# The second layer's gate and up gemms of a two-block transformer kernel, 256 tokens per matmul instead of 512

## What is computed

```python
h = rmsnorm(x, norm2_g[i]) * (1.0 + sc2) + sh2
x = x + g2 * swiglu(h, w_gate[i], w_up[i], w_down[i])

def swiglu(h, w_gate, w_up, w_down):
    return (jax.nn.silu(h @ w_gate) * (h @ w_up)) @ w_down
```

## Time and profile before

| What | Value |
|---|---|
| Median of 3 runs | 2285.78 us |
| Lowest and highest | 2285.34 us, 2288.35 us |
| Profiled execution, first to last instruction (its span) | 2283.5 us |
| PE busy | 2243.0 us, 98% of the span |
| PEld (weight loads) busy | 1801.7 us, 79% |
| DVE busy | 1190.3 us, 52% |
| ACT busy | 897.0 us, 39% |
| POOL busy | 164.5 us, 7% |
| Mean granted TensorE clock | 0.996 of full speed |

### The profile page before, as it was taken

How to read it: one execution, slowest core, us unless ns; L and a number is a source line. 1 busy time by engine, 2 the same in 40 slices (tenths; PEclk the granted TensorE clock), 3 DMA queues, 4 the chain that set the end, 5 groups by cost and what they waited for, 6 DMA issues and landing times. The chain is left out here.

```text
span 2283.5 us, 27109 instructions
## 1 busy us (share of the span) xinstructions
PE 2243.0 (98%) x11012; PEld 1801.7 (79%) x11012; DVE 1190.3 (52%) x1642; ACT 897.0 (39%) x1446; POOL 164.5 (7%) x147
## 2 busy tenths in 40 slices
PE   7999999999999999999999999999999999999998
PEld 4767788888777778888888878887788888888886
DVE  4765755543465754333336546567752346553453
ACT  3664322232354533322234236377653224331331
POOL 2112000000100010000001001032110001000001
PEclk9999999999999999999999999999999999999999
DMA  9322555532211122222222324333233222323222
GB/s 347 129 102 103 196 206 216 203 111 102 84 65 65 56 74 84 101 93 93 101 92 83 111 84 139 118 109 111 97 103 122 90 102 84 110 87 107 93 83 83
DMA packets 82172, 259.11 MB, mean 113 GB/s; under 512 B 8800, under 2 KB 17248, under 8 KB 82048
## 3 DMA queue, kind: packets, MB, share of 16 engines
q1 hardware_dynamic: 82048, 257.38, 32.6%
HBM read 253.09 MB, written 4.26 MB: 113 GB/s over the span
## 5 line engine op out<-in xcount | busy, mean ns | idle before, releaser
L850 PE MATMUL pb<-hhi,whi 128*128 128x512 f32 x1944 | 771.8, 397 | 3.0 <-ACT hhi L1263 3.0
L852 PE MATMUL pb<-hhi,wlo 128*128 128x512 f32 x1944 | 757.9, 390 | 2.3 <-DVE wlo L1534 2.3
L854 PE MATMUL pb<-hlo,whi 128*128 128x512 f32 x1944 | 758.5, 390 | 0.0
L1534 DVE TENSOR_TENSOR wlo<-raw,whi 128x1024 fp32r<-128x1024 f32 x361 | 446.5, 1241 | 536.4 <-ACT whi L1225 536.2
L1225 ACT ACTIVATE whi<-raw 128x1024 fp32r<-128x1024 f32 x361 | 380.2, 1057 | 699.2 <-PE pb L854 679.1
L850 PEld LDWEIGHTS pb<-hhi,whi 128*128 128x128 f32 x1944 | 365.0, 188 | 90.7 <-issue 17.2
L852 PEld LDWEIGHTS pb<-hhi,wlo 128*128 128x128 f32 x1944 | 365.3, 188 | 79.1 <-DVE wlo L1534 3.1
L854 PEld LDWEIGHTS pb<-hlo,whi 128*128 128x128 f32 x1944 | 364.8, 188 | 78.8 <-DVE hlo L1631 0.9
L850 PE MATMUL pb<-ahi,whi 128*128 128x512 f32 x848 | 335.0, 395 | 1.4 <-ACT ahi L1421 0.7
L852 PE MATMUL pb<-ahi,wlo 128*128 128x512 f32 x848 | 330.9, 390 | 1.1 <-DVE wlo L1534 1.1
L854 PE MATMUL pb<-alo,whi 128*128 128x512 f32 x848 | 331.3, 391 | 0.0
(11 more groups left out here) (251 smaller groups left out, 1730.4 us busy)
## 6 DMA issues: line engine op xcount, KB each, us to landing
raw<-stream SPq DMA_DIRECT2D x361, 512.0 KB, 3.2
slab<-ada_w SPq DMA_DIRECT2D x80, 512.0 KB, 5.1
early<-ada_w SPq DMA_DIRECT2D x32, 256.0 KB, 8.6
slab<-sums SPq DMA_DIRECT2D x32, 256.0 KB, 4.3
X<-xT SPq DMA_DIRECT2D x8, 256.0 KB, 5.1
ya<-slab SPq DMA_DIRECT2D x8, 256.0 KB, 4.5
slab<-ya SPq DMA_DIRECT2D x8, 256.0 KB, 5.8
outT<-X SPq DMA_DIRECT2D x8, 256.0 KB, 2.1
```

Source lines behind the costliest of these rows:

```text
L850: e.matmul(out, wh, hi, start=s.k == 0, stop=False)
L852: e.matmul(out, wl, hi, start=False, stop=False)
L854: i = e.matmul(out, wh, lo, start=False, stop=s.last)
L1534: e.tensor_tensor(wlo[:, u % NW, :], raw[:, u % NRAW, :], whi[:, u % NW, :].bitcast(F), ALU.subtract).then_inc(*v_cut.up(u))
```

## The change

For sources with the key `("h", 3, k)` the three matmuls of a product become six. Each of the three is issued twice with the same weights, first for tokens 0 to 255 (`left`) and then for tokens 256 to 511 (`right`), into the two halves of the same bank. Only the left matmul of the first slice begins a new sum (`start`); the right one of the first slice has `start=False`. The waits stand where they stood: ahead of the first, the third and the fifth of the six. The semaphore goes up with the sixth. All other products are unchanged.

```diff
--- before.py
+++ after.py
@@ -847,11 +847,22 @@
             wh, wl, out = whi[:, at, sl], wlo[:, at, sl], b[:s.rows, :]
             w.wait_ge(a_cut, s.u)
             w.wait_ge(a_half, s.src)
-            e.matmul(out, wh, hi, start=s.k == 0, stop=False)
-            w.wait_ge(v_cut, s.u)
-            e.matmul(out, wl, hi, start=False, stop=False)
-            w.wait_ge(v_half, s.src)
-            i = e.matmul(out, wh, lo, start=False, stop=s.last)
+            if s.src[:2] == ("h", 3):
+                left, right = slice(0, 256), slice(256, 512)
+                e.matmul(out[:, left], wh, hi[:, left], start=s.k == 0, stop=False, skip_group_check=True)
+                e.matmul(out[:, right], wh, hi[:, right], start=False, stop=False, skip_group_check=True)
+                w.wait_ge(v_cut, s.u)
+                e.matmul(out[:, left], wl, hi[:, left], start=False, stop=False, skip_group_check=True)
+                e.matmul(out[:, right], wl, hi[:, right], start=False, stop=False, skip_group_check=True)
+                w.wait_ge(v_half, s.src)
+                e.matmul(out[:, left], wh, lo[:, left], start=False, stop=s.last, skip_group_check=True)
+                i = e.matmul(out[:, right], wh, lo[:, right], start=False, stop=s.last, skip_group_check=True)
+            else:
+                e.matmul(out, wh, hi, start=s.k == 0, stop=False)
+                w.wait_ge(v_cut, s.u)
+                e.matmul(out, wl, hi, start=False, stop=False)
+                w.wait_ge(v_half, s.src)
+                i = e.matmul(out, wh, lo, start=False, stop=s.last)
             done = [("tile", s.tile)] * s.last + [("unit", s.u)] * (s.b == 7) + [("used", s.src)] * s.frees
             if done:
                 i.then_inc(*t_mm.up(*done))
```

## The result

| | Before | After |
|---|---|---|
| Median of 4 runs | 2285.59 us | 2297.16 us |
| Lowest and highest | 2285.34, 2288.35 us | 2295.72, 2300.16 us |
| Ratio | | 1.0059, 95% interval 1.0047 to 1.0071 |
| Span of the profiled execution | 2283.5 us | 2294.7 us |

The account below looks back on a forecast made before the run. TensorE was taken to bound the touched stages; 1,056 added matmuls at 13.3 ns give +14.1 us, so 2283.5 becomes 2297.6 us of span and the median 2299.9 us. Range of 8 in 10: 2284 to 2310 us.

Parts of the forecast that it names:

- That TensorE is the bound in both stages: Second layer's gate and up stages, 859 to 990 and 1056 to 1164 us: PE never idle, each nanosecond reaches the end.
- 1,056 added matmuls, each with a load of its own: Second layer's gate and up products: 1,056 matmuls of 512 columns become 2,112 of 256, adding 1,056 weight loads.
- 13.3 ns for each, taken from 226.7 - 213.3: Touched matmuls: time not explained by columns at 2.4 GHz, taken as per instruction; 120 ns a half, +14.1 us.
- The rows that I argued from: Earlier trace's transposes, ordinary loads and side-by-side 128-column matmuls: 7 and 5 ns left over, taken to favour cost per instruction.
- The loads stay hidden, with 8 ns to spare, and a floor of 112 ns: Weight loads in the touched stages: following each other every 112 ns, below 120 a half; lower bound -2.9 us.
- Other engines covered: Touched stages: ScalarE waits 163.4 us for TensorE, VectorE 150.2 us for ScalarE, so a slower PE gives them slack.
- The sum: Whole program: 2283.5 + 14.1 = 2297.6 us of span, median 2299.9 us, 0.6% more; chance 0.58.
- The column rival: Moving operand's read, 4 bytes a column: cost belongs to columns, 113.3 ns a half, 0 to 3 us; chance 0.25.
- The upset pace: Touched matmuls: closer loads start each 5.3 ns late, or issue takes 124 to 126 ns; 2309 to 2311 us; chance 0.12.
- Fully exposed loads: Weight loads of the touched matmuls not hidden at all: 188 ns a half, +158 us, 2443 us; chance 0.02.
- The Trainium skill's rule: Distance of two warm matmuls: columns over 2.4 GHz and 2.5 ns, 215.8 ns for 512 columns; 2.6 us in all.

Follow-up runs that it names:

- the quarters: Kernel before, with the second layer's gate and up products issued as four matmuls of 128 tokens instead of one of 512: 2517.08 us, +232.8.

## Why the prediction was right, point by point

- **That TensorE is the bound in both stages, so each nanosecond arrives at the end.** Right. The two stages grew by 14.0 us, PE is not idle in them, and the quarters passed 232.8 us on to the end.
- **1,056 added matmuls, each with a load of its own.** Right: 12,068 instructions on PE and on PEld.
- **13.3 ns for each, taken from 226.7 - 213.3.** Right as a number: 120.0 ns a half, 240.0 a pair. The reason behind it, a fixed cost of the instruction, is only half borne out. For fp32r with 128 weight columns it is the same at 256 and 512 tokens, which was all that the sum needed. But it is not the instruction's own: it falls to 2.5 ns with bf16 operands and changes with the width of the weights; with 64 weight columns it is not even the same at the two lengths, 6.6 and 16.7 ns. That it is the same with 128 was argued from rows that do not show it, and is in part luck: 256 columns take 106.7 ns, less than the 112 of a load, and no run excludes that the load has a hand in the 120 ns. The rows that I argued from, to the earlier trace rows, are reads of other kinds, and the 7 and 5 ns left over there were no measure of this one.
- **The loads stay hidden, with 8 ns to spare, and a floor of 112 ns.** Right, and shown by the two runs that went below it: 111.7 ns in quarters, 286.7 ns for 384 and 128.
- **Other engines covered.** Right, ScalarE's wait for PE grew by 11 us.
- **The sum.** 14.1 us forecast, 14.0 in the stages, 13.5 by the ratio of the runs, 11.6 by the medians. What the profiled pair lacks lies ahead of the stages, in code that is the same, largely at another granted clock.
- **The column rival** fell: no stretch at 113 ns with full weights. **The upset pace** did not come: the halves run at 120.0 ns throughout. It exists, though: 32 and 64 weight columns at 512 tokens show 232 and 230 on average. **Fully exposed loads** (188 ns) came nowhere, the floor of 112 came with the quarters. **The Trainium skill's rule** of columns over 2.4 GHz and 2.5 ns (page TensorE: Matmul & The Clock Gate, section Back-to-back issue gap), by which the change would cost an estimated 2.6 us, holds for bf16 to within 0.2 ns at both lengths (215.7 and 109.2 ns), and does not hold for fp32r, where 13.3 ns were measured in place of 2.5. The 131 ns that the same section of the Trainium skill gives for 512 columns in a stream with loads appeared in no run.

## What to carry to other kernels

Take the cost of splitting a matmul from the distance of starts in the trace, less its columns at full clock, and only from the operand type in question: here 13.3 ns in fp32r and some 2.7 in bf16. Then look at the weight load behind it: no part should be so short that its columns and its share together take less than the load needs, 112 ns for 128 fp32r columns (parts of 128 columns were too short here, parts of 256 were not, and none between was tried). An uneven split with one short part cost four times an even one with as many instructions. And where such a share stands beside every matmul of a program that TensorE bounds, the operand type can be worth more than the shape: 4.4% of the time here, against 0.6% for the split, if the bits can be spared.

## What the runs showed of the hardware that I had not expected

- A matmul of 512 fp32r columns takes 226.7 ns and one of 512 bf16 columns 215.8, both with a 128-column load beside them, at a granted clock of 1.00 (2.4 GHz). So in this stream fp32r stays 6% short of one column per cycle at 2.4 GHz. At 1.2 GHz it reached one column per cycle, with 512 columns (427 ns) and with 256 (213 ns).
- Narrower weights can make a matmul of the same moving columns slower: 230.0 ns with 64 weight columns against 226.7 with 128, at 512 tokens, in means of distances between 224 and 236, while at 256 tokens they make it faster, 113.3 against 120.0. Open.
- Two executions of the same code ahead of the stage differed by 2.8 us, with a granted clock of 0.50 in one of them from 150.9 to 154.3 us and again from 857.4 to 860.8 us, and of 1.00 in the other.
- By the profile's records, a matmul can start while its own load is still under way: with 384 and 128 columns in turn, 0.06 us behind the start of a load that lasts 0.19.
